# A banded attention's turns, and the last projection group's quarters, moved in the second block's written order

## The reference, cut to what matters

```python
h = _rms(x, norm1)
z = h @ w_in                                   # 1024 x 2572, f32
(aq, ak, av, bq, bk, bv, bf, cq, ck, cv, ci, cf, co) = _split_in_proj(z)
ya = _swa_attention(_rope(_rms(aq)), _rope(_rms(ak)), av, sinks)   # 8 heads, banded mask
yb = _fox_attention(_rms(bq), _rms(bk), bv, log_sigmoid(bf))       # 4 heads, decay added to the scores
yc = sigmoid(co) * _rms(_mlstm(cq, ck, cv, ci, cf))                # 4 heads, exp(decay) times the scores
x = x + concat(ya, yb, yc) @ w_out
x = x + square(relu(_rms(x, norm2) @ w_ff1)) @ w_ff2
```

## Time and profile before

| | us |
|---|---|
| median of 3 runs (1708.62 to 1717.09) | 1711.74 |
| profiled execution, its own time | 1707.9 |
| its span | 1706.6 |
| TensorE busy in the span | 1603.4 (94%) |
| VectorE busy | 828.6 (49%) |
| ScalarE busy | 670.1 (39%) |
| mean granted TensorE clock | 0.983 of full |

### The profile page before, as it was taken

One profiled execution on the slowest core, in us unless ns is written; L12 is line 12 of the kernel. 1 busy time (PEld: TensorE's weight loads), 2 busy tenths in 40 slices (PEclk: granted clock), 3 DMA queues, 4 the chain that ended last, 5 costly groups with the idle time before them and its releaser, 6 DMA issues. The chain is left out here.

```text
span 1706.6 us, 22915 instructions
## 1 busy us (share of the span) xinstructions
PE 1603.4 (94%) x9612; PEld 1228.9 (72%) x9612; DVE 828.6 (49%) x1428; ACT 670.1 (39%) x1035; POOL 31.2 (2%) x53
## 2 busy tenths in 40 slices
PE   6999999999879899999999989899999999999999
PEld 5788998544333778899744333478899987789998
DVE  6666565301001757656611010487555558755554
ACT  5355543111011544544211111357454446745443
POOL 5000000000000000000000000000000000000000
PEclk9999999999989999999999999998999999899999
DMA  9542457879999434244869999643355544335552
GB/s 310 166 149 101 147 188 299 326 294 422 421 373 391 175 132 169 103 162 184 344 272 359 421 421 419 279 155 117 130 191 189 182 172 150 124 124 190 181 196 99
DMA packets 58405, 393.75 MB, mean 231 GB/s; under 512 B 7437, under 2 KB 7453, under 8 KB 14125
## 3 DMA queue, kind: packets, MB, share of 16 engines
q1 hardware_dynamic: 55008, 381.35, 58.6%
q0 software_dynamic: 3136, 9.50, 1.9%
q10 hardware_dynamic: 144, 1.30, 0.2%
HBM read 391.07 MB, written 1.05 MB: 230 GB/s over the span
## 5 line engine op out<-in xcount | busy, mean ns | idle before, releaser
L1767 DVE TENSOR_TENSOR ring_rounded<-ring_sb,ring_rounded 128x2048 fp32r<-128x2048 f32 (+3 forms) x180 | 385.5, 2154 | 198.9 <-ACT ring_rounded L1370 198.5
L1370 ACT ACTIVATE ring_rounded<-ring_sb 128x2048 fp32r<-128x2048 f32 (+3 forms) x180 | 322.5, 1804 | 167.0 <-PE psum L602 143.9
L602 PE MATMUL psum<-ring_sb,region_sb 128*64 128x512 f32 x1440 | 335.3, 605 | 32.7 <-DMA ring_sb<-in_weights 20.2
L602 PE MATMUL psum<-xT_hi_rounded,ring_rounded 128*128 128x256 f32 x1920 | 349.3, 283 | 0.0
L602 PEld LDWEIGHTS psum<-xT_hi_rounded,ring_rounded 128*128 128x128 f32 x1920 | 299.7, 192 | 0.7
L602 PE MATMUL psum<-ring_rounded,region_rounded 128*128 128x512 f32 x1184 | 288.0, 393 | 0.0
L602 PEld LDWEIGHTS psum<-ring_sb,region_sb 128*64 128x64 f32 x1440 | 108.7, 139 | 235.4 <-issue 233.0
L602 PE MATMUL psum<-xT_lo_rounded,ring_rounded 128*128 128x256 f32 x960 | 275.2, 287 | 0.5 <-DVE ring_rounded L1767 0.5
L602 PEld LDWEIGHTS psum<-ring_rounded,region_rounded 128*128 128x128 f32 x1184 | 222.2, 189 | 47.0
L602 PE MATMUL psum<-ring_rounded,xT_hi_rounded 128*128 128x512 f32 (+4 forms) x832 | 232.1, 356 | 16.7 <-DVE ring_rounded L1767 14.1
L602 PEld LDWEIGHTS psum<-xT_lo_rounded,ring_rounded 128*128 128x128 f32 x960 | 184.5, 192 | 3.4 <-issue 2.5
(11 more groups left out here) (263 smaller groups left out, 1295.3 us busy)
## 6 DMA issues: line engine op xcount, KB each, us to landing
ring_sb<-in_weights SPq DMA_DIRECT2D x328, 1024.0 KB, 7.0
ring_sb<-in_weights SPq DMA_DIRECT2D x16, 768.0 KB, 4.4
region_sb<-in_weights SPq DMA_DIRECT2D x6, 1024.0 KB, 10.0
ring_sb<-in_weights SPq DMA_DIRECT2D x8, 584.0 KB, 9.8
ring_sb<-in_weights SPq DMA_DIRECT2D x4, 536.0 KB, 4.7
region_sb<-in_mem_turned POOLq DMA_DIRECT2D x2, 1024.0 KB, 7.1
region_sb<-in_pool_band POOLq DMA_DIRECT2D x2, 1024.0 KB, 9.1
region_sb<-in_ln_g POOLq DMA_DIRECT2D x4, 512.0 KB, 5.4
```

The source lines that it names most:

```text
L602: return nc.tensor.matmul(dst, lhsT, rhs, start=first, stop=last, skip_group_check=True)
L1370: nc.scalar.activation(rounded(piece.hi), piece.raw, ACT.Copy).then_inc(hi_made, 1)
L1767: nc.vector.tensor_tensor(rounded(piece.raw), piece.raw, reread(piece.hi), ALU.subtract).then_inc(lo_made, 1)
```

## The change

On TensorE: `turn_swa` moves one quarter later (from before to behind the third quarter of group 3), the banded scores of b = 0 and b = 1 move from behind the third and fourth quarter of group 3 to behind the first and second of group 4, and `turn_others` from the middle of group 4 to its fourth quarter. `swa_probs(0)` leaves `turn_others` and stands behind group 4. The four quarters of group 5 stood as two pairs; now the first stands behind `pe_fox_scores(l, 0)`, the second behind `pe_swa_values(l, 0)`, the third behind `pe_fox_scores(l, 1)`, the fourth behind the scores of the memory attention. The order in which the banks are taken stays.

On ScalarE: the copies of `swa_probs(0)` move from ahead of the exponentials of the banded attention's b = 1 to behind `cut(4)`, and group 5 is copied out two steps later. On VectorE: the remainder of one weight piece (`round_lo(first + 15)` becomes 14) moves behind the last scores.

```diff
@@ tensor_second, turn_others
                 pe_turn(("fox_k", l), fox["turned"][:, :, 256:512], 256, [fox_qk_made.at(l, 1)], fox_normed.at(l))
-                swa_probs(0)
@@ tensor_second
-            cut(3, between=turn_swa, amid=lambda: pe_swa_scores(l, 0))
-            pe_swa_scores(l, 1)
-            cut(4, turn_others)
+            def second_gates():
+                pe_mls_gates(l, 1)
+                pe_swa_values(l, 0)
+
+            def second_scores():
+                swa_probs(1)
+                pe_fox_scores(l, 1)
+
+            def memory_scores():
+                pe_mls_scores(l, 0)
+                pe_mls_scores(l, 1)
+
+            cut(3, amid=turn_swa)
+            cut(4, early=lambda: pe_swa_scores(l, 0), between=lambda: pe_swa_scores(l, 1), amid=turn_others)
+            swa_probs(0)
             pe_mls_gates(l, 0)
             pe_fox_scores(l, 0)
-            pe_mls_gates(l, 1)
-            pe_swa_values(l, 0)
-            cut(5, lambda: swa_probs(1))
-            pe_fox_scores(l, 1)
-            pe_mls_scores(l, 0)
-            pe_mls_scores(l, 1)
+            cut(5, early=second_gates, between=second_scores, amid=memory_scores)
             pe_swa_values(l, 1)
@@ scalar_second
-            act_probs(("swa_probs", l, 0), SWA_HEADS, 1, swa_room, swa_turned)
             act_exps(swa["probs"][1], SWA_HEADS, S, softmax_stats("swa", 1, SWA_HEADS), swa_lowered.at(l, 1), 1.0, swa_exped)
             act_sink(l, 1)
             cut(4)
+            act_probs(("swa_probs", l, 0), SWA_HEADS, 1, swa_room, swa_turned)
...
             act_y(l, 0, 0)
+            round_hi(first + 14)
             act_probs(("swa_probs", l, 1), SWA_HEADS, 2, swa_room, swa_turned)
-            cut(5)
+            round_hi(first + 15)
             act_mls_weights(l, 1)
             act_exps(fox["probs"][1], FOX_HEADS, S, softmax_stats("fox", 1, FOX_HEADS), fox_lowered.at(l, 1), 1.0, fox_exped)
+            cut(5)
@@ vector_second
-            round_lo(first + 15)
+            round_lo(first + 14)
```

## The result

Before, the median of six runs is 1707.7 us (1704.78 to 1717.09); after, 1723.17 us (1718.88 to 1727.98). The ratio is 1.0072, with a 95% interval of 1.0047 to 1.0097: 12.3 us slower, 8 to 17 us. The profiled execution took 1718.88 us.

A forecast was written before the change was run, and what follows sets the result against it. TensorE, busy nearly throughout, was taken as the bound. Per layer 5.7 - 0.3 + 1.0 + 0.3 = 6.7 us, 13.4 us for two (5 to 23), on 1711.7 us gives 1725 us; 8-in-10 range 1716 to 1736 us.

The forecast's parts named there:

- fox keys' transposes later: TensorE, layer 0: the decay rows that release these transposes come 2.2 us later, at 1161.8 us.
- wait for the decay rows: TensorE ahead of the fox keys' transposes: waits 3.1 us in place of 0.9 us, spending the quarter won.
- ScalarE's row up to the copies: ScalarE from the fox keys' copy to the end of the `swa_probs(0)` copies: 10.3 us without a break.
- fox scores later: First fox scores on TensorE start 5.7 us later per layer, bounds 5.0 and 6.4 us.
- wait for the copies: TensorE ahead of the first fox scores: waits 6.3 us for ScalarE's copies of `swa_probs(0)`.
- fox scores to `swa_probs(1)`: TensorE stretch, per layer: 0.3 us less from group 5's quarters, 1.0 us more for fox scores at the low clock.
- `swa_probs(1)` to the output product: Last TensorE stretch of the part: 0.3 us more per layer, bounds 1.5 us less and 1.5 us more.
- third move: Copies of `swa_probs(0)` behind group 4 on ScalarE: said to decide the sum, fox scores 5.7 us later.
- second move: Banded scores a quarter later: scores slip 2.8 us, decay rows 2.2 us, spending the quarter won.
- The low clock: Rival, chance 0.20: 1.2 GHz from the new wait up to the output product, 23.4 us more in all, 1735 us.
- The clock gains: Rival, chance 0.13: same wait, clock back at once, no second fall at 1187 us; 3.3 us a layer, 1718 us.
- case of a win: Rival, chance 0.05: ScalarE reaches the copies by 1167 us, no new wait, 4.0 us a layer won, 1704 us.

The follow-up runs named there:

- second profile: Both kernels profiled once more, unchanged: the kernel before took 1722.55 us, the changed kernel 1723.99 us.

## Why the prediction was right

The forecast was 1725 us, from 13.4 us more; measured were 1723.17 us, and 12.3 us more by the ratio. By its own steps, from the first profiles (the terms of the sum are the fox scores and the last two):

| step, per layer | on record | measured, layer 0 |
|---|---|---|
| wait for the rotated heads that stays | 0.3 us | 0.3 us |
| fox keys' transposes later | 2.2 us | 21.07 - 19.05 = 2.0 us |
| wait for the decay rows | 3.1 us | 2.9 us |
| ScalarE's row up to the copies | 10.3 us | 10.3 us |
| fox scores later | 5.7 us | 5.7 us |
| wait for the copies | 6.3 us | 4.7 us (6.3 in one layer of the second profile) |
| fox scores to `swa_probs(1)` | + 0.7 us | + 2.9 us |
| `swa_probs(1)` to the output product | + 0.3 us | - 1.2 us |
| sum | 6.7 us | 7.4 us (7.0 in layer 1) |

**The mechanism was right.** The third move decides: alone it costs 10.6 us, for 12.3 us of the whole change, and taken back it leaves no loss. The rest, 1.7 us, is smaller than the intervals. In the profile the second move adds to the third by starting ScalarE's row 2 us later (layer 0: 5.7 us of shift for both, 3.7 us for the third move alone: 30.26 - 26.55); that this is the rest of the time is argued, not shown.

**The wait was mis-sized, the shift was not.** I let TensorE run the last quarter of group 4 in 2.8 us; behind the 2.9 us wait it ran at half clock, and TensorE arrived 1.6 us later. That cost nothing, because the end of the wait is ScalarE's. The second profile shows both sizes of the wait with the same end.

**The clock's terms were mis-sized and partly cancelled.** This is the step that the prediction had most wrong: from the fox scores to `swa_probs(1)` it had 0.7 us more, and it was 2.9 us in the first profile, 2.2 and 2.5 us in the second. For the fox scores at the low clock I took 1.0 us. Measured, from the fox scores to VectorE's read of the gates it is 1177.80 - 1169.66 = 8.14 us, less the quarter in front of the gates, 2.9 us, 5.3 us, where it was 3.4: 1.9 us. The two quarters took 2.9 and 2.7 us, for 4.9 us together before, and the rest of the 2.9 us is the gates and the quarters' starts. In the second profile this stretch ends with the wait for VectorE's division, 1.74 and 1.73 us, which the text on record had weighed for the full clock. In the last stretch I had 0.3 us more and it became 1.2 us less, since the clock stayed full there in this execution; in the second profile the same stretch is 1.5 us more (18.4 us) and 0.1 us less. These two terms are not properties of the kernel alone but of where the clock falls.

**The rivals.** The low clock (1735 us) did not come in full: the clock was low for 16 us in a row from the wait on, more than before, but came back ahead of the second fox scores. "The clock gains" (1718 us) has one half right in the first profile, where the fall at 1187 us was gone; in the second the clock fell once more behind `swa_probs(1)` in both layers. The case of a win needed a row of ScalarE under 4.5 us; the experiment that puts the copies ahead of group 4's shows what it looks like (no wait), but the gain beside it, 2 us with an interval from 6 us less to 2 us more, can't be told from nothing and is less than the 8 us worked out: the wait for the decay rows stays at 2.9 us and the clock is low for 13.7 us of the part in each layer.

**What the sum took for granted** was that the first profile stands for the kernel. It was 4.4 us a layer shorter in this part than the second, and the step worth 5.7 us a layer in the first pair of profiles is worth 1.4 and 2.5 us in the second. So the closeness of the total (13.4 us for 12.3) is in part luck: the times come from many executions, and the sum was made from one profile, with clock terms that came out too small in one stretch and too large in the other. The forecast in microseconds was helped as well by a base of 1711.7 us, 4.0 us above the later median of 1707.7, while the medians lie 15.5 us apart and not 13.4.

## What to carry to other kernels

Where small products share banks in turn, look up for each moved step who takes its bank next and which engine frees it: a copy put a few steps later in another engine's row is a wait that ends with that row. A step that fills a wait should leave the steps that feed the busier engine where they were; `turn_swa` put a quarter later with the same quarters between it and the scores was 0.6% faster; with one more quarter between them it won 0.2%, with an interval that ends at nothing. Predict when a wait ends, rather than how long it is. And take a second profile before a step of a few microseconds is read from one: here two profiles of one program differed by 4.4 us a layer.

## What the runs showed of the hardware

The same program's clock fell at other places from one execution to the next: behind a wait of 3.06 us it went to 1.2 GHz in one profile (0.50 from 1147 to 1154 us) and not in the other, where 18 us at the full clock followed. The first and the last of its stretches of 1 us behind the 3.11 us wait in layer 0, columns as in the earlier trace rows:

```profile
1140.58:1141.58 1.00, 1.00 (x9) 1.00 (x10) 1.00 (x1) 0.00 (x0) 0.00 (x0) 1.00 0.00 0
...
1157.58:1158.58 1.00, 1.00 (x11) 0.93 (x9) 1.00 (x2) 0.67 (x2) 0.00 (x0) 1.00 0.33 49
```

All those between are at 1.00 too. A fox score pair of small products, 64 rows by 128 columns, took 0.48 us at the full clock and 0.76 us at the low one; the ten fill-in products of constants took 0.46 us each, and the clock was 1.00 over them. With this work in the pause the clock fell some microseconds later, at 0.72 from 1170 to 1182 us, but it still fell.
